# Layer norm inside a two-block network: squares about a provisional mean of four blocks, shifted by GpSimd while the last two blocks are made

## The chip, the cores and the metric

The kernel runs on one core of a Trainium2 chip. The metric is the time of one execution on the device, in microseconds (us). It is 1038.09 us, the median of 3 runs (1037.78 to 1038.72). The engines are named as the profile names them: PE is TensorE (PEld its weight loads), DVE is VectorE, ACT is ScalarE, POOL is GpSimd, SP is SyncE.

## The reference, cut to what matters

The program is a Conformer convolution block, a differential attention block with their SwiGLU and gate layers, and a second block of three branches, for 256 tokens of 1024 features in float32. The change lies in the convolution module of the first block, in its layer norm over the 1024 features:

```
def layer_norm(x, g, b):
    xf = x.astype(jnp.float32)
    mu = jnp.mean(xf, axis=-1, keepdims=True)
    xc = xf - mu
    var = jnp.mean(xc * xc, axis=-1, keepdims=True)
    y = xc * lax.rsqrt(var + EPS) * g.astype(jnp.float32) + b.astype(jnp.float32)
    return y.astype(x.dtype)

def conformer_conv(x, w_pw1, b_pw1, dw_w, dw_b, ln_g, ln_b, w_pw2, b_pw2):
    a = x @ w_pw1 + b_pw1
    u = a[..., :D_MODEL] * jax.nn.sigmoid(a[..., D_MODEL:])
    u = lax.conv_general_dilated(...)            # causal depthwise, 31 taps
    u = jax.nn.silu(layer_norm(u, ln_g, ln_b))
    return u @ w_pw2 + b_pw2
```

## The kernel before, in words

Every matrix product of float32 inputs is made of three products of rounded halves: `w_hi` and `w_lo` for a weight piece, `x_hi`, `x_lo` or `z_hi`, `z_lo` for the data (function `mm3`, lines L276 to L278). Weights come as 169 pieces of 1 MB, fetched by SP into `raw`, rounded by ACT into `w_hi` (L906) and subtracted by DVE into `w_lo` (L1388); for pieces 2 to 10 and two later ones POOL makes the low half (L795, `low`). The order of each engine is written out by hand, and engines wait for each other on counting semaphores.

In the convolution module the features lie on the 128 partitions, in 8 blocks of 128 features (f = 0 to 7), each block 256 tokens wide. Blocks 0 to 3 of the depthwise convolution are made by DVE, tap by tap (`taps_on_vector`, L1583 to L1594, the last add of a block is L1594). Blocks 4 to 7 are made by PE in four column strips of 32 (`conv_taps`, L476: 32 matmuls for a block, two recorded instructions each), and ACT copies them out with their bias (`conv_out`, L1057). All land in `y` (8 blocks).

The layer norm needs sums over the features, which lie on partitions, so PE makes them with a constant matrix `inv_d` (all 1/1024), which leaves the sum on all partitions. Before, this goes:

- POOL adds blocks 0, 1, 4 and 2 into `y_part`; PE multiplies `y_part` (L499) and blocks 5, 6, 3, 7 (`mean_of`, L486) into bank 0, which then holds the mean.
- DVE subtracts the mean from all of `y` in place, two blocks at a time (L1611).
- ACT squares `y` into `sq` (L1107); PE sums the squares in four column strips of bank 7 (L513); DVE copies them out to `y_sums` (L1615); two matmuls with one column turn the strips' sums into the variance of 128 tokens each (L521); DVE adds EPS (L1618); POOL raises to -0.5 (L835); DVE multiplies the identity by it (`y_diag`, L1621); PE spreads it over the partitions (`y_row`, L527).
- DVE multiplies `y` by that row (`scaled`, L1627), ACT applies gain, bias and SiLU (L1115) and rounds to `z_hi` (L1120), DVE makes `z_lo` (`v_split`, L1635). This runs over five groups of blocks, BLOCKS = (0), (1), (2,3), (4,5), (6,7).
- PE starts the second pointwise product (`by_feature`, piece 9) and waits ahead of each group for its `v_split`.

Between these steps PE does work that waits for nothing here: the four parts of the projection `proj0` (`projection_part`, two 128-row blocks of three matmuls each), and six transposes that nobody reads (`keep_warm`, L443). POOL, after `low(10)`, adds the bias row of the second product to `h` in four pieces of 128x512 (L827), starts the DMA of the attention bias (`toep`, L832), and then waits for the variance.

Of the kernel before, what the change touches and what calls it, by code (L numbers as in the profile page):

```python
# [77 lines left out]
def build(nc, ws, x_tok, p_feat, par, rows, lam_rows, rel, onehot, sgu_w, pool_m, toep, u_scr, out):  # L78
    ctx = ExitStack()
    with ctx:  # L80
# [46 lines left out]
        y_odd = view(9968, 2, SEQ)  # L127
        u_pad = view(2272, 7, PADDED)
# [120 lines left out]
        def _(pe):  # L249
# [30 lines left out]
            def tok(ap, k, t):  # L280
                return ap[:, k, t * P:(t + 1) * P]
# [61 lines left out]

            def projection_part(layer, g, b, t, n):

                begin(b)
                for k in range(2):
                    c = slice(k * D + n * 512, k * D + (n + 1) * 512)
                    ins = mm3(banks[b][:, :], tok(z_hi, KB - 2 + k, t), tok(z_lo, KB - 2 + k, t),
                              w_hi[:, g % SPLIT, c], w_lo[:, g % SPLIT, c], k == 0, k == 1)  # L350
                end(("proj", layer, t, n), b, ins, g if t == 1 and n == 1 else None)
# [128 lines left out]
            def mean_of(f, last=False):  # L480

                if f < CONV_PE:
                    pe.wait_ge(S("conv"), f + 1)
                else:
                    pe.wait_ge(S("conv_pe"), f - CONV_PE + 1)
# [10 lines left out]
            conv_taps(6)  # L496
# [3 lines left out]
            mean_of(5)  # L500
            conv_taps(7)
            mean_of(6)
            mean_of(3)
            mean_of(7, last=True)
            pe.wait_ge(S("p_split"), 1)
            lo_ready(pe, G["proj0"])
            for n in range(2):
                projection_part(0, G["proj0"], (1, 4)[n], 0, n)
            begin(7)
            for f in range(KB):  # L510
                pe.wait_ge(S("y_sq"), f // 2 + 1)
                j = f % QUADS
                ins = pe.matmul(banks[7][j * LANE:(j + 1) * LANE, 0:SEQ], inv_d[:, 0:LANE], sq[:, f, :],  # L513
                                start=f < QUADS, stop=f >= QUADS)
            end("squares", 7, ins, release=(S("y_sums"), 1))
            pe.wait_ge(S("y_sums"), 1)
            pe.wait_ge(S("one_32nd"), 1)
            begin(3)
            begin(2)
            for t, b in enumerate((3, 2)):  # L520
                end(("var", t), b, pe.matmul(banks[b][:, 0:1], y_sums[:, t * P:(t + 1) * P], one_32nd, start=True, stop=True),  # L521
                    release=(S("y_var"), t + 1))
            projection_part(0, G["proj0"], 5, 1, 0)
# [5 lines left out]
            projection_part(0, G["proj0"], 6, 1, 1)  # L529
            keep_warm(6, 7)  # L530
# [230 lines left out]
        def _(pool):  # L761
# [62 lines left out]
            for n_ in range(2):  # L824
                for t in range(TT):
                    c = slice(n_ * 512, (n_ + 1) * 512)
                    pool.tensor_tensor(h[:, t, c], h[:, t, c], row_b2[:, c], ALU.add).then_inc(S("h_biased"), 1)  # L827


            pool.wait_ge(S("bias_row"), 2)  # L830
            pool.wait_ge(S("ld_u0"), 128)
            pool.dma_start(toep, bias_row[:, :].unsqueeze(1).to_broadcast([HEADS, P, 384])).then_inc(S("toep_out"), 16)  # L832
            pool.memset(one_32nd, 1.0 / LANE).then_inc(S("one_32nd"), 1)
            pool.wait_ge(S("y_var"), 2)
            pool.tensor_tensor(st[:, 84:86], st[:, 82:84], st2[:, 56:58], ALU.pow).then_inc(S("y_r"), 1)  # L835
            pool.wait_ge(S("h_done"), 4)
# [59 lines left out]
        def _(act):  # L896
# [204 lines left out]
            spread(7)  # L1101
            conv_out(5)
            conv_out(6)
            conv_out(7)
            for f in range(4):
                act.wait_ge(S("centred"), f + 1)
                act.activation(sq[:, 2 * f:2 * f + 2, :], y[:, 2 * f:2 * f + 2, :], ACT.Square).then_inc(S("y_sq"), 1)  # L1107
# [263 lines left out]
        def _(dve):  # L1371
# [234 lines left out]
            bank, free = take(dve, "mean")  # L1606
            dve.wait_ge(S("conv_pe"), KB - CONV_PE)
            dve.wait_ge(S("conv"), CONV_PE)
            for i in range(4):
                k = slice(2 * i, 2 * i + 2)  # L1610
                dve.tensor_tensor(y[:, k, :], y[:, k, :], bank[:, 0:SEQ].unsqueeze(1).to_broadcast([P, 2, SEQ]),  # L1611
                                  ALU.subtract).then_inc(S("centred"), 1)
# [3 lines left out]
            for t in range(TT):  # L1616
                bank, free = take(dve, ("var", t))
                dve.tensor_scalar(st[:, 82 + t:83 + t], bank[:, 0:1], 1.0, EPS, ALU.mult, ALU.add).then_inc(S("y_var"), 1)  # L1618
# [4 lines left out]
            dve.wait_ge(S("centred"), 4)  # L1623

            def scaled(i):
                k = slice(*BLOCKS[i])
                dve.tensor_tensor(y[:, k, :], y[:, k, :],  # L1627
# [10 lines left out]
            for i in range(3):  # L1638
                scaled(i)
            v_split(0)  # L1640
# [451 lines left out]
```

## Time and profile before

| what | value |
|---|---|
| median of 3 runs | 1038.09 us (1037.78 to 1038.72) |
| the profiled execution | 1037.69 us, of which the span of instructions is 1035.9 us |
| PE busy | 1024.0 us, 99% |
| DVE busy | 640.8 us, 62% |
| ACT busy | 519.3 us, 50% |
| POOL busy | 107.8 us, 10% |
| granted clock of TensorE, mean | 0.999 |

The span counts from the first to the last instruction; the profiled execution has 1.8 us around it. Times in a timeline count from the start of the span. A row of the timeline may merge several instructions of one line (x3), and the durations of matmuls overlap, since they are pipelined: how far PE moves in a stretch is read from the start of one row to the start of the next. A number in square brackets is the idle time of the engine ahead of the row and what ended it.

### The profile page before, as it was taken

To read this page: it belongs to the slowest core of one execution; us is meant where nothing else is said; L and a number is where in the kernel's file an instruction comes from. 1 tells how busy PE (TensorE), PEld (TensorE's weight loads), DVE (VectorE), ACT (ScalarE), POOL (GpSimd) and SP (SyncE) were. 2 spreads that over 40 slices of the span, in tenths; PEclk is the share of its full clock that TensorE was granted. 3 is DMA by queue.
4 is the path that set the end of the run, shared out by engine and by line. 5 is a ranking of instruction groups with operands and counts; after the bars stand their busy time and mean duration, and the time that the engine had idled before them with its cause. 6 is when DMAs were issued, how large, how long until landed. Compare 5 with 4: busy or idle time off the path is not lost.

```text
span 1035.9 us, 13552 instructions
## 1 busy us (share of the span) xinstructions
PE 1024.0 (99%) x5530; PEld 865.2 (84%) x5530; DVE 640.8 (62%) x802; ACT 519.3 (50%) x635; POOL 107.8 (10%) x87
## 2 busy tenths in 40 slices
PE   8999999999999999999999999999999999999997
PEld 7977888888888888888888888788888888999886
DVE  5996745445457667765454456676454557777564
ACT  6337544434466668654434346754544454344433
POOL 4991100000020320010000002100000000000000
PEclk9999999999999999999999999999999999999999
DMA  8766865555453632565455554555545445454531
GB/s 311 254 186 129 259 224 191 192 179 197 174 192 122 230 137 82 204 225 202 175 191 196 177 196 163 210 202 214 198 179 190 159 163 203 172 195 164 205 120 41
DMA packets 30669, 191.67 MB, mean 185 GB/s; under 512 B 3720, under 2 KB 6280, under 8 KB 8720
## 3 DMA queue, kind: packets, MB, share of 16 engines
q1 hardware_dynamic: 25056, 179.06, 48.1%
q0 software_dynamic: 2096, 7.79, 3.3%
q10 hardware_dynamic: 3456, 3.97, 1.3%
q8 instruction: 44, 0.72, 0.3%
q14 instruction: 17, 0.14, 0.0%
HBM read 187.58 MB, written 3.21 MB: 184 GB/s over the span
## 4 chain that ended last, share of the span: by engine, by line
PE 98%; DVE 1%; ACT 0%; issue 0%; POOL 0%; POOLq 0%; ACTq 0%
PE bank L276 30%; PE bank L278 30%; PE bank L277 30%; PE bank L318 2%; PE bank L476 1%; PE bank L393 1%; PE bank L450 1%; PE bank L570 0%; PE bank L667 0%; PE bank L704 0%; DVE w_lo L1388 0%; PE bank L591 0%; PE bank L486 0%; DVE arena L1433 0%; DVE x_lo L1443 0%
## 5 line engine op out<-in xcount | busy, mean ns | idle before, releaser
L1388 DVE TENSOR_TENSOR w_lo<-raw,w_hi 128x2048 fp32r<-128x2048 f32 x158 | 361.7, 2292 | 210.9 <-ACT w_hi L906 210.6
L906 ACT ACTIVATE w_hi<-raw 128x2048 fp32r<-128x2048 f32 x169 | 322.7, 1910 | 162.3 <-PE bank L278 151.5
L276 PE MATMUL bank<-w_hi,x_hi 128*128 128x512 f32 x800 | 317.7, 397 | 0.2
L278 PE MATMUL bank<-w_hi,x_lo 128*128 128x512 f32 x800 | 312.5, 391 | 0.0
L277 PE MATMUL bank<-w_lo,x_hi 128*128 128x512 f32 x800 | 311.5, 389 | 0.0
L276 PEld LDWEIGHTS bank<-w_hi,x_hi 128*128 128x128 f32 x800 | 150.2, 188 | 34.4 <-issue 3.9
L278 PEld LDWEIGHTS bank<-w_hi,x_lo 128*128 128x128 f32 x800 | 150.1, 188 | 32.4
L277 PEld LDWEIGHTS bank<-w_lo,x_hi 128*128 128x128 f32 x800 | 150.4, 188 | 29.2
L276 PE MATMUL bank<-w_hi,z_hi 128*128 128x512 f32 (+1 forms) x368 | 143.4, 390 | 0.1
L278 PE MATMUL bank<-w_hi,z_lo 128*128 128x512 f32 (+1 forms) x368 | 141.7, 385 | 0.0
L277 PE MATMUL bank<-w_lo,z_hi 128*128 128x512 f32 (+1 forms) x368 | 141.5, 385 | 0.0
L276 PE MATMUL bank<-x_hi,w_hi 128*128 128x256 f32 x384 | 108.9, 284 | 1.5 <-DVE x_lo L1443 1.5
L277 PE MATMUL bank<-x_lo,w_hi 128*128 128x256 f32 x384 | 108.7, 283 | 0.0
L278 PE MATMUL bank<-x_hi,w_lo 128*128 128x256 f32 x384 | 108.7, 283 | 0.0
L795 POOL TENSOR_TENSOR w_lo<-raw,w_hi 128x2048 fp32r<-128x2048 f32 x11 | 51.1, 4650 | 370.1 <-ACT w_hi L906 370.1
L276 PEld LDWEIGHTS bank<-w_hi,z_hi 128*128 128x128 f32 x368 | 69.2, 188 | 14.1 <-issue 0.8
L278 PEld LDWEIGHTS bank<-w_hi,z_lo 128*128 128x128 f32 x368 | 69.1, 188 | 13.9
L277 PEld LDWEIGHTS bank<-w_lo,z_hi 128*128 128x128 f32 x368 | 69.2, 188 | 13.1
L276 PEld LDWEIGHTS bank<-x_hi,w_hi 128*128 128x128 f32 x384 | 73.7, 192 | 2.3 <-DVE x_lo L1443 1.1
L277 PEld LDWEIGHTS bank<-x_lo,w_hi 128*128 128x128 f32 x384 | 73.7, 192 | 0.0
L278 PEld LDWEIGHTS bank<-x_hi,w_lo 128*128 128x128 f32 x384 | 73.7, 192 | 0.0
L963 ACT ACTIVATE z_hi<-bank 128x512 fp32r<-128x512 f32 x22 | 13.1, 597 | 75.6 <-PE bank L393 75.6
(224 smaller groups left out, 757.6 us busy)
## 6 DMA issues: line engine op xcount, KB each, us to landing
raw<-in_ws SPq DMA_DIRECT2D x169, 1024.0 KB, 4.8
arena<-u_scr ACTq DMA_DIRECT2D x16, 142.0 KB, 4.6
arena<-in_rows POOLq DMA_DIRECT2D x2, 1024.0 KB, 5.1
toep<-bias_row POOLq DMA_DIRECT2D x1, 1536.0 KB, 34.4
h<-in_x_tok SPq DMA_DIRECT2D x2, 512.0 KB, 4.9
arena<-in_rows POOLq DMA_DIRECT2D x2, 512.0 KB, 5.9
arena<-toep POOLq DMA_DIRECT2D x1, 1024.0 KB, 11.0
arena<-in_pool_m POOLq DMA_DIRECT2D x1, 768.0 KB, 4.7
```

The lines of the kernel that those rows point to most:

```text
L276: pe.matmul(dst, s_hi, m_hi, start=first, stop=False)
L277: pe.matmul(dst, s_hi, m_lo, start=False, stop=False)
L278: return pe.matmul(dst, s_lo, m_hi, start=False, stop=last)
L318: ins = pe.transpose(banks[b][:, k * P:(k + 1) * P], src[:, k * P:(k + 1) * P], ident[:, :])
L393: ins = pe.transpose(banks[b][:, k * SEQ + t * P:k * SEQ + (t + 1) * P], hid[:, t, k * P:(k + 1) * P], ident[:, :])
L450: pe.matmul(banks[b][:, 0:P], ones[:, :], ident[:, :], start=True, stop=True)
L476: ins = pe.matmul(banks[b][j * LANE:(j + 1) * LANE, 0:SEQ], taps_of[:, i, q, j, :], u_rows[i % 3][:, j, 4 * q:4 * q + SEQ], start=q == 0, ...
L795: pool.tensor_tensor(w_lo[:, g % SPLIT, :], raw[:, g % RAW, :], w_hi[:, g % SPLIT, :].bitcast(F32), ALU.subtract).then_inc(S("lo_pool"), 1)
L906: act.activation(w_hi[:, g % SPLIT, :], raw[:, g % RAW, :], ACT.Copy).then_inc(hi_done, 1)
L963: act.activation(z_hi[:, k0:k0 + 2, :], bank[:, :].rearrange("p (k s) -> p k s", k=2), ACT.Copy).then_inc(S("t_hi"), 1)
L1388: dve.tensor_tensor(w_lo[:, g % SPLIT, :], raw[:, g % RAW, :], w_hi[:, g % SPLIT, :].bitcast(F32), ALU.subtract).then_inc(lo_done, 1)
```

## The change

The squares are no longer taken about the mean but about a pivot, and the difference is taken out afterwards. The pivot is the mean over four blocks: PE multiplies `y_part` twice (1/1024 each, over 512 features). ACT copies it to `pivot_row`. POOL subtracts it from blocks 0,1 then 2, then 4,5, then 6 (`shift`), DVE from 3 and 7. ACT squares each group as it is shifted. PE sums the shifted blocks (the mean of what is left, e, in bank 2) and the squares (bank 7), in an order that follows the shifts. The variance is the mean of squares less e squared: two more matmuls with one column (`e_cols`), a squaring on ACT and one DVE instruction that subtracts (`scalar_tensor_tensor`, two columns at once). DVE subtracts e from `y` (`centre`, four times) in between the later steps, instead of all ahead of the squares. POOL's four additions to `h` (`add_b2`) go from ahead of its power to behind it. `sq` lies at another place, `projection_part` is cut into steps of three matmuls, and `keep_warm` has 2 transposes for 6.

```
-        sq = view(6384, KB, SEQ)
+        sq = view(0, KB, SEQ)
...
-            def mean_of(f, last=False):
...
-                ins = pe.matmul(banks[0][:, 0:SEQ], inv_d, y[:, f, :], start=False, stop=last)
+            def mean_of(f, shifted, first=False, last=False):
+
+                pe.wait_ge(*shifted)
+                if first:
+                    begin(2)
+                ins = pe.matmul(banks[2][:, 0:SEQ], inv_d, y[:, f, :], start=first, stop=last)
                 if last:
-                    end("mean", 0, ins, release=(S("centred"), 4))
+                    end("mean", 2, ins, release=(S("centred"), 4))
+
+            def square_of(f, squared, last=False):
+
+                pe.wait_ge(S("y_sq"), squared)
+                j = f % QUADS
+                ins = pe.matmul(banks[7][j * LANE:(j + 1) * LANE, 0:SEQ], inv_d[:, 0:LANE], sq[:, f, :],
+                                start=f not in square_seen, stop=f in square_seen)
+                square_seen.update((f, (f + QUADS) % KB))
+                if last:
+                    end("squares", 7, ins, release=(S("y_sums"), 1))
...
             conv_taps(5)
-            conv_taps(6)
             begin(0)
             pe.wait_ge(S("y_part"), 1)
             pe.matmul(banks[0][:, 0:SEQ], inv_d, y_part, start=True, stop=False)
-            mean_of(5)
+            end("pivot", 0, pe.matmul(banks[0][:, 0:SEQ], inv_d, y_part, start=False, stop=True),
+                release=(S("shifted_v"), 2))
+            conv_taps(6)
             conv_taps(7)
-            mean_of(6)
-            mean_of(3)
-            mean_of(7, last=True)
             pe.wait_ge(S("p_split"), 1)
             lo_ready(pe, G["proj0"])
-            for n in range(2):
-                projection_part(0, G["proj0"], (1, 4)[n], 0, n)
+            projection_step(0, G["proj0"], 1, 0, 0, 0)
+            projection_step(0, G["proj0"], 1, 0, 0, 1)
+            mean_of(5, (S("shifted"), 3), first=True)
+            mean_of(6, (S("shifted"), 4))
             begin(7)
-            for f in range(KB):
...
+            square_of(0, 1)
+            square_of(1, 1)
+            square_of(2, 2)
+            square_of(4, 3)
+            square_of(5, 3)
+            square_of(6, 4)
+            mean_of(3, (S("shifted_v"), 1))
+            mean_of(7, (S("shifted_v"), 2), last=True)
+            square_of(3, 5)
+            square_of(7, 6, last=True)
+            projection_step(0, G["proj0"], 4, 0, 1, 0)
+            begin(0)
+            pe.wait_ge(S("e_row"), 1)
+            pe.wait_ge(S("one_32nd"), 1)
+            for t in range(TT):
+                ins = pe.matmul(banks[0][:, t:t + 1], e_row[:, t * P:(t + 1) * P], one_32nd, start=True, stop=True)
+            end("e_cols", 0, ins, release=(S("e_sq"), 1))
+            begin(3)
             pe.wait_ge(S("y_sums"), 1)
...
+            projection_step(0, G["proj0"], 4, 0, 1, 1)
+            projection_step(0, G["proj0"], 5, 1, 0, 0)
+            projection_step(0, G["proj0"], 5, 1, 0, 1)
             begin(3)
             pe.wait_ge(S("y_diag"), 2)
...
-            projection_part(0, G["proj0"], 6, 1, 1)
-            keep_warm(6, 7)
+            projection_step(0, G["proj0"], 6, 1, 1, 0)
+            projection_step(0, G["proj0"], 6, 1, 1, 1)
+            keep_warm(2, 7)
...
+            def shift(f0, f1):
+
+                pool.tensor_tensor(y[:, f0:f1, :], y[:, f0:f1, :], pivot_row.unsqueeze(1).to_broadcast([P, f1 - f0, SEQ]),
+                                   ALU.subtract).then_inc(S("shifted"), 1)
...
             low(10)
+            pool.wait_ge(S("pivot_row"), 1)
+            shift(0, 2)
+            shift(2, 3)
...
+            shift(4, 6)
...
+            shift(6, 7)
...
+            pool.wait_ge(S("y_var"), 1)
+            pool.tensor_tensor(st[:, 84:86], st[:, 82:84], st2[:, 56:58], ALU.pow).then_inc(S("y_r"), 1)
             pool.wait_ge(S("ld_b2"), 16)
             pool.wait_ge(S("x_scaled_1"), 1)
             pool.wait_ge(S("x_scaled"), 1)
...
+            add_b2(0)
+            add_b2(1)
...
+            square(0, 2, (S("shifted"), 1))
+            square(2, 3, (S("shifted"), 2))
             conv_out(7)
...
+            square(4, 6, (S("shifted"), 3))
+            square(6, 7, (S("shifted"), 4))
+            square(3, 4, (S("shifted_v"), 1))
+            square(7, 8, (S("shifted_v"), 2))
+            bank, _ = take(act, "mean")
+            act.activation(e_row, bank[:, 0:SEQ], ACT.Copy).then_inc(S("e_row"), 1)
+            bank, _ = take(act, "e_cols")
+            act.activation(st2[:, 50:52], bank[:, 0:TT], ACT.Square, scale=LANE / P).then_inc(S("e_sq"), 1)
             table(ACT.Silu)
```

On DVE the same part reads, in the changed kernel:

```
            dve.scalar_tensor_tensor(out=st[:, 82:84], in0=bank[:, 0:TT], scalar=EPS, in1=st2[:, 50:52], op0=ALU.add,
                                     op1=ALU.subtract).then_inc(S("y_var"), 1)
...
            centre(0)
            dve.wait_ge(S("y_r"), 1)
            for t in range(TT):
                dve.tensor_scalar(y_diag[:, t, :], ident[:, :], st[:, 84 + t:85 + t], None, ALU.mult).then_inc(S("y_diag"), 1)
            centre(1)
            row, free = take(dve, "y_row")
...
            for i in range(3):
                scaled(i)
            centre(2)
            v_split(0)
            scaled(3)
            centre(3)
            v_split(1)
            scaled(4)
```

How the instructions stand on the engines, row by row. PE before, from the sums of squares to the variance and the next projection matmuls (L513 squares, L521 variance):

```order
L513 MATMUL bank<-arena 32x256 x8
L521 MATMUL bank<-st,arena 128x1 x2
L276 MATMUL bank<-w_hi,z_hi 128x512
L277 MATMUL bank<-w_lo,z_hi 128x512
L278 MATMUL bank<-w_hi,z_lo 128x512
```

PE in the changed kernel, the same place (L492 sums of shifted blocks, L500 squares, L543 `e_cols`, L548 variance; lines are those of the changed kernel):

```order
L492 MATMUL bank<-arena 128x256 x2
L500 MATMUL bank<-arena 32x256 x6
L492 MATMUL bank<-arena 128x256 x2
L500 MATMUL bank<-arena 32x256 x2
L277 MATMUL bank<-w_hi,z_hi 128x512
L278 MATMUL bank<-w_lo,z_hi 128x512
L279 MATMUL bank<-w_hi,z_lo 128x512
L543 MATMUL bank<-st,arena 128x1 x2
L548 MATMUL bank<-st,arena 128x1 x2
```

The eight squares are cut into six and two with full-width sums between, and three projection matmuls and two one-column matmuls now stand ahead of the variance.

DVE before, from the last block of the convolution to the second `v_split`:

```order
L1594 TENSOR_TENSOR arena<-bank,arena 128x256
L1611 TENSOR_TENSOR arena<-arena,bank 128x512 x4
L1615 COPY arena<-bank 128x256
L1618 TENSOR_SCALAR st<-bank 128x1 x2
L1621 TENSOR_SCALAR arena<-ident,st 128x128 x2
L1627 TENSOR_TENSOR arena<-arena,bank 128x256 x2
L1627 TENSOR_TENSOR arena<-arena,bank 128x512
L1635 TENSOR_TENSOR z_lo<-arena,z_hi 128x256
L1627 TENSOR_TENSOR arena<-arena,bank 128x512
L1635 TENSOR_TENSOR z_lo<-arena,z_hi 128x256
```

DVE in the changed kernel (L1670, L1672 subtract the pivot, L1681 is `centre`, L1694 `y_diag`, L1701 `scaled`, L1709 `v_split`):

```order
L1670 TENSOR_TENSOR arena<-arena,bank 128x256
L1672 TENSOR_TENSOR arena<-arena,bank 128x256
L1675 COPY arena<-bank 128x256
L1686 SCALAR_TENSOR_TENSOR st<-bank,st 128x2
L1681 TENSOR_TENSOR arena<-arena,bank 128x512
L1694 TENSOR_SCALAR arena<-ident,st 128x128 x2
L1681 TENSOR_TENSOR arena<-arena,bank 128x512
L1701 TENSOR_TENSOR arena<-arena,bank 128x256 x2
L1701 TENSOR_TENSOR arena<-arena,bank 128x512
L1681 TENSOR_TENSOR arena<-arena,bank 128x512
L1709 TENSOR_TENSOR z_lo<-arena,z_hi 128x256
L1701 TENSOR_TENSOR arena<-arena,bank 128x512
```

The third subtraction of a mean now stands ahead of the first `v_split`, the fourth (not shown) ahead of the second.

POOL before, behind the third addition to `y_part` (L795 is `low(10)`, L827 the additions to `h`, L835 the power):

```order
L795 TENSOR_TENSOR w_lo<-raw,w_hi 128x2048
L827 TENSOR_TENSOR h<-h,arena 128x512 x4
L832 DMA toep<-bias_row 1024x1x384
L833 MEMSET st 128x1
L835 TENSOR_TENSOR st<-st 128x2
```

POOL in the changed kernel (L825 is `low(10)`, L859 `shift`, L876 the power, L855 `add_b2`):

```order
L825 TENSOR_TENSOR w_lo<-raw,w_hi 128x2048
L859 TENSOR_TENSOR arena<-arena 128x512
L859 TENSOR_TENSOR arena<-arena 128x256
L859 TENSOR_TENSOR arena<-arena 128x512
L859 TENSOR_TENSOR arena<-arena 128x256
L873 DMA toep<-bias_row 1024x1x384
L876 TENSOR_TENSOR st<-st 128x2
L855 TENSOR_TENSOR h<-h,arena 128x512 x4
```

The four shifts take the place of the four additions, and the additions now start where the power ends.

## Rows read from the trace of the kernel before

**Rows 1.** The page, the chain that ended last, shares of the span

```profile
PE 98%; DVE 1%; ACT 0%; issue 0%; POOL 0%; POOLq 0%; ACTq 0%
```

**Rows 2.** Stretches: us, busy (instructions) of PE, PEld, DVE, ACT, POOL, then PEclk, DMA

```profile
0.00:40.00 40.00, 35.99 (x280) 34.50 (x281) 27.85 (x53) 21.48 (x22) 24.29 (x22) 1.00 0.82 288
...
82.00:90.00 8.00, 7.30 (x48) 5.16 (x47) 4.20 (x11) 5.77 (x11) 0.83 (x2) 1.00 0.49 52
```

**Rows 3.** Timeline of PE around the layer norm: start, us, what

```profile
79.43 1.68 PE L486 MATMUL bank<-arena 128*128 128x256 f32 x6
80.76 0.58 PE L276 MATMUL bank<-w_hi,z_hi 128*128 128x512 f32 x1
...
83.77 1.21 PE L513 MATMUL bank<-arena 128*32 128x256 f32 x16
85.50 0.61 PE L521 MATMUL bank<-st,arena 128*128 128x1 f32 x4 [0.53 <-DVE arena L1615]
85.97 0.47 PE L276 MATMUL bank<-w_hi,z_hi 128*128 128x512 f32 x1
...
87.78 0.68 PE L527 MATMUL bank<-arena,ones 128*128 128x128 f32 x4 [0.18 <-DVE arena L1621]
88.22 0.48 PE L276 MATMUL bank<-w_hi,z_hi 128*128 128x512 f32 x1
...
89.68 0.82 PE L443 MATMUL bank<-ident 128*128 128x128 f32 x6
90.64 0.47 PE L276 MATMUL bank<-w_hi,z_hi 128*128 128x512 f32 x1
```

**Rows 4.** Timeline of DVE around the layer norm

```profile
79.50 0.42 DVE L1594 TENSOR_TENSOR arena<-bank,arena 128x256 f32<-128x256 f32 x1
81.15 2.48 DVE L1611 TENSOR_TENSOR arena<-arena,bank 128x512 f32<-128x512 f32 x4 [1.22 <-PE bank L486]
...
87.15 0.48 DVE L1621 TENSOR_SCALAR arena<-ident,st 128x128 f32<-128x128 f32 x2 [0.85 <-POOL st L835]
88.50 1.35 DVE L1627 TENSOR_TENSOR arena<-arena,bank 128x256 f32<-128x256 f32 x3 [0.86 <-PE bank L527]
90.11 0.43 DVE L1635 TENSOR_TENSOR z_lo<-arena,z_hi 128x256 fp32r<-128x256 f32 x1 [0.26 <-ACT z_hi L1120]
...
91.05 0.43 DVE L1635 TENSOR_TENSOR z_lo<-arena,z_hi 128x256 fp32r<-128x256 f32 x1
```

**Rows 5.** Timeline of POOL around the layer norm and after it

```profile
75.89 5.00 POOL L827 TENSOR_TENSOR h<-h,arena 128x512 f32<-128x512 f32 x4
...
86.39 0.73 POOL L835 TENSOR_TENSOR st<-st 128x2 f32<-128x2 f32 x1 [4.29 <-DVE st L1618]
...
118.20 0.72 POOL L849 TENSOR_TENSOR st<-st 128x2 f32<-128x2 f32 x1
```

**Rows 6.** Timeline of ACT behind the first block scaled

```profile
88.95 0.60 ACT L1115 ACTIVATE arena<-arena,prm 128x256 f32<-128x256 f32 x1 [2.17 <-DVE arena L1627]
```

**Rows 7.** Timeline of DVE at 8, 118 and 341 us

```profile
8.99 2.30 DVE L1548 TENSOR_SCALAR arena<-h,st 128x1024 f32<-128x1024 f32 x1 [7.11 <-POOL st L783]
...
118.27 1.29 DVE L1443 TENSOR_TENSOR x_lo<-arena,x_hi 128x512 fp32r<-128x512 f32 x2
...
340.84 2.29 DVE L1388 TENSOR_TENSOR w_lo<-raw,w_hi 128x2048 fp32r<-128x2048 f32 x1
```

**Rows 8.** Timeline of POOL at 8 us

```profile
8.11 0.73 POOL L783 TENSOR_TENSOR st<-st 128x2 f32<-128x2 f32 x1
8.83 4.23 POOL L787 TENSOR_TENSOR arena<-arena,prm 128x1024 f32<-128x1024 f32 x2
```

**Rows 9.** One line each: duration in ns, min/median/max, first and last start

```profile
L787 POOL TENSOR_TENSOR arena<-arena,prm x4: 1904/1929/2356, 8.8 to 55.7; 128x1024 f32<-128x1024 f32 x4
L858 POOL TENSOR_SCALAR arena<-st x4: 204/208/2207, 341.0 to 384.9; 128x16 f32<-128x16 f32 x4
L1960 DVE TENSOR_SCALAR arena<-arena,st x1: 486/486/486, 1032.2 to 1032.2; 128x512 f32<-128x512 f32 x1
```

More of the change, by code:

```diff
@@ L509, in _ @@
+            projection_step(0, G["proj0"], 1, 0, 0, 1)
+            mean_of(5, (S("shifted"), 3), first=True)
+            mean_of(6, (S("shifted"), 4))
             begin(7)
-            for f in range(KB):
[L511 to L515, printed above, removed]
@@ L516, in _ @@
-            pe.wait_ge(S("y_sums"), 1)
[L517 to L523, printed above, removed]
+            square_of(0, 1)
+            square_of(1, 1)
+            square_of(2, 2)
+            square_of(4, 3)
@@ L524, in _ @@
+            end("e_cols", 0, ins, release=(S("e_sq"), 1))
+            begin(3)
+            pe.wait_ge(S("y_sums"), 1)
+            for t in range(TT):
+                ins = pe.matmul(banks[3][:, t:t + 1], y_sums[:, t * P:(t + 1) * P], one_32nd, start=True, stop=True)
+            end("var", 3, ins, release=(S("y_var"), 1))
+            projection_step(0, G["proj0"], 4, 0, 1, 1)
+            projection_step(0, G["proj0"], 5, 1, 0, 0)
+            projection_step(0, G["proj0"], 5, 1, 0, 1)
             begin(3)
@@ L823, in _ @@
             pool.wait_ge(S("x_scaled"), 1)
[L824 to L835, printed above, removed]
+            add_b2(0)
+            add_b2(1)
             pool.wait_ge(S("h_done"), 4)
@@ L1101, in _, with square @@
             spread(7)
+            bank, _ = take(act, "pivot")
+            act.activation(pivot_row, bank[:, 0:SEQ], ACT.Copy).then_inc(S("pivot_row"), 1)
             conv_out(5)
             conv_out(6)
-            conv_out(7)
-            for f in range(4):
-                act.wait_ge(S("centred"), f + 1)
-                act.activation(sq[:, 2 * f:2 * f + 2, :], y[:, 2 * f:2 * f + 2, :], ACT.Square).then_inc(S("y_sq"), 1)
+            def square(f0, f1, shifted):
+                act.wait_ge(*shifted)
+                act.activation(sq[:, f0:f1, :], y[:, f0:f1, :], ACT.Square).then_inc(S("y_sq"), 1)
+            square(0, 2, (S("shifted"), 1))
+            square(2, 3, (S("shifted"), 2))
+            conv_out(7)
+            square(4, 6, (S("shifted"), 3))
[6 more added lines that the diff above has]
+            act.activation(st2[:, 50:52], bank[:, 0:TT], ACT.Square, scale=LANE / P).then_inc(S("e_sq"), 1)
             table(ACT.Silu)
@@ L1605, in _ @@
             taps_on_vector(3, {4: lambda: gated(7)})
-            bank, free = take(dve, "mean")
+            bank, free = take(dve, "pivot")
+            dve.wait_ge(S("pivot_row"), 1)
+            dve.wait_ge(S("conv"), CONV_PE)
+            dve.tensor_tensor(y[:, 3, :], y[:, 3, :], bank[:, 0:SEQ], ALU.subtract).then_inc(S("shifted_v"), 1)
             dve.wait_ge(S("conv_pe"), KB - CONV_PE)
[L1608 to L1612, printed above, removed]
+            dve.tensor_tensor(y[:, 7, :], y[:, 7, :], bank[:, 0:SEQ], ALU.subtract).then_inc(S("shifted_v"), 1)
             feed(9)
@@ L1615, in _, with centre @@
             dve.tensor_copy(y_sums, bank[:, 0:SEQ]).then_inc(S("y_sums"), 1)
-            for t in range(TT):
-                bank, free = take(dve, ("var", t))
-                dve.tensor_scalar(st[:, 82 + t:83 + t], bank[:, 0:1], 1.0, EPS, ALU.mult, ALU.add).then_inc(S("y_var"), 1)
+            e_bank, _ = take(dve, "mean")
+            def centre(i):
+                k = slice(2 * i, 2 * i + 2)
+                dve.tensor_tensor(y[:, k, :], y[:, k, :], e_bank[:, 0:SEQ].unsqueeze(1).to_broadcast([P, 2, SEQ]),
+                                  ALU.subtract).then_inc(S("centred"), 1)
+            bank, free = take(dve, "var")
+            dve.wait_ge(S("e_sq"), 1)
+            dve.scalar_tensor_tensor(out=st[:, 82:84], in0=bank[:, 0:TT], scalar=EPS, in1=st2[:, 50:52], op0=ALU.add,
+                                     op1=ALU.subtract).then_inc(S("y_var"), 1)
+            dve.wait_ge(S("e_row"), 1)
+            dve.wait_ge(S("shifted"), 4)
+            dve.wait_ge(S("shifted_v"), 2)
+            centre(0)
             dve.wait_ge(S("y_r"), 1)
```

32 lines of the change are left out of this document (22 added, 10 removed).

## The prediction

> **What bounds the kernel now.** I read the page first, its chain of work that ended last: 98% of the span is PE [rows 1]. So the time changes only where PE's own work changes or where PE waits, and the change lies in one stage, from 79.43 us (PE has finished the convolution) to 90.64 us (PE starts the second pointwise product) [rows 3]. The reader is to see how little PE loses there: it is busy 7.30 of the 8.00 us between 82 and 90 [rows 2]. It waits 0.53 us for the copy of the sums of squares, 0.18 us at `y_row`, and from 89.68 to 90.64 us, 0.96 us, it runs the filler transposes and then waits for the first `v_split`, which ends at 90.11 + 0.43 = 90.54 us [rows 3, 4]. With all of PE's idle time in 82 to 90 (0.70 us) the stage has at most 0.70 + 0.96 = 1.7 us to give. That is under 0.2% of 1038 us (2.1 us), which is about what a measurement of this kernel can tell from no change. So the question is mostly what the change adds. Last I read POOL and DVE side by side, since POOL's work is moved.
>
> **The pivot and the shifts.** Two matmuls for the pivot stand where `y_part` and block 5 stood, so block 7 of the convolution still ends near 79.43 us. Behind `low(10)` POOL makes four shifts. The additions took 5.00 / 4 = 1.25 us for 128x512, from 75.89 us [rows 5]; I take 1.25 for a shift of two blocks and 0.75 for one, so the last ends at 75.9 + 4.0 = 79.9 us. DVE ends block 3 at 79.92 us [rows 4] and shifts blocks 3 and 7, 0.42 each, by 80.8. ACT's squares (0.6 for two blocks) follow by 81.8. PE wants the last of these only after 83 us (below). All this is hidden, with over 1 us of cover. POOL's DMA `toep` starts 0.9 us earlier, with a reader far away: hidden.
>
> **PE from 79.43 us to `y_row`.** Sums of blocks: three took 80.76 - 79.43 = 1.33 us, so four take 1.77. Projection: still 18 matmuls ahead of `y_row`, twelve at 83.77 - 80.76 = 3.01 us and six at 89.68 - 88.22 = 1.46: 4.47. Squares: a full-width sum is two recorded halves of 1.33 / 6 = 0.22 us. Eight in four strips took 1.21 us with their tail, their sixteen halves started over 0.83 us, so a strip takes 0.22 a half and four strips run side by side. Now six run in three strips (four halves deep, 0.89 us) and two, blocks 3 and 7, in one and the same strip (four halves one behind the other, 0.89 us): 1.78. `e_cols` and the variance: 85.97 - 85.50 = 0.47 each, 0.94. Four more changes between strips and full width: twelve projection matmuls between two other kinds took 0.09 us more than twice six, so 0.36. The sum is 9.32 us, `y_row` at 88.75 us against 87.78 [rows 3]: 0.97 later. If the one strip costs nothing extra and the changes are free, it is 1.25 less. The waits of PE are gone, but they were 0.7 us, and the added work is more.
>
> **The variance chain, without POOL's other work.** `y_row` less nine projection matmuls (2.19) less 0.47 puts the variance at 86.09 us. Before, POOL's power started 86.39 - 85.50 = 0.89 us behind it and took 0.73, DVE started 0.03 later and took 0.48 for both `y_diag` [rows 3 to 5]. So: power 86.98 to 87.71 us, `y_diag` until 88.22, PE could start at 88.37, and its own queue (88.75) ends later. `centre(0)` lies under the power. ACT has 2.17 us of idle ahead of the first SiLU [rows 6]; its table load and copies move 2 us later and just fit.
>
> **What POOL now does beside `y_diag`.** This is the step I rest the forecast on. The four additions to `h` now start right behind the power, the moment in which `y_diag` starts on DVE. The same meeting stands in the trace at 8.8 us: a power ends (L783), POOL goes straight on to L787, and DVE starts L1548, released by that same power [rows 7, 8]. L1548 takes 2.30 us for 128x1024. The same operation takes 0.486 us for 128x512, late in the program with POOL idle, and POOL's first L787 ends at about 8.83 + 1.9 = 10.7 us; DVE's instruction ends at 11.29 [rows 7 to 9]. So it stood still until POOL's had ended and then ran 0.55 us. The second L787 took 2.36 us where the median is 1.93, so POOL in turn waited for DVE [rows 9]. It happens the other way too: L858 takes 0.2 us, and 2.21 where it started inside DVE's L1388, which has two inputs in SBUF and ends at 343.13 us, as L858 does within 0.1 [rows 7, 9]. Against it stands one row: DVE's L1443 at 118.27 us, two SBUF inputs, started inside POOL's power L849 and was not delayed (1.29 for two) [rows 5, 7]; but a power of 2 columns reads almost nothing.
>
> The Trainium skill, page "SBUF — State Buffer", section "SBUF: two separate sides", states that VectorE and GpSimd share a port pair as an exclusive lock for a whole instruction, for a VectorE operation in a 2-port mode or with two SBUF inputs. The trace agrees at 8.8 and 341 us, and not at 118 us. By the page the sum is the one that follows; by the row at 118 us alone it would be the first rival's.
>
> With it: POOL's first addition starts at 87.7 us and ends at 88.97. The first `y_diag` ends 0.15 us later, about 89.1. POOL's second addition is already queued and takes its turn, until 90.37; the second `y_diag` ends at 90.5, PE's `y_row` starts at 90.67. From `y_row` to the second product it was 90.64 - 87.78 = 2.86 us. `centre(2)` (2.48 / 4 = 0.62) now stands ahead of the first `v_split`, of which 0.35 lay idle from one start to the next: 0.27 more. PE starts the product at 93.80, 3.16 us later. The second `v_split` came 91.05 - 90.11 = 0.94 us behind the first, now 1.56 with `centre(3)`, against 1.4 of PE's work: about 0.1 more [rows 3, 4]. Later ones have slack. Sum 3.2 us. If both `y_diag` slip in behind the first addition, `y_row` is at 89.45, the first `v_split` is wanted at 92.04 and meets the fourth addition (until 93.05): product at 93.45, 2.8 us. I take 3.0. Behind the stage PE is never short of work for 300 us, so nothing is given back.
>
> Made against the profiled execution, 1037.69 us (1035.9 of span and 1.8 around it), this gives 1040.7; that execution lies 0.4 under the median of 1038.09, so I forecast **1041.1 us**.
>
> **The rivals.**
> *No meeting of POOL and DVE* (this is the other side, no slower that can be told). Then `y_row` is at 88.75, the product at 88.75 + 2.86 + 0.27 = 91.88, 1.24 later, and 1.35 with the second `v_split`: 1039.4. For it: the row at 118 us, and that POOL's loop may start its reads after DVE's short instruction (128 columns) is through. It decides whenever both `y_diag` and the `v_split`s end unstretched.
> *Only the `v_split`s meet it.* Both `y_diag` win, at 88.2; the additions then end at 89.5, 90.7, 92.0 and 93.2, the first `v_split` (wanted at 91.34) ends at 92.3, the second behind the fourth: 1.9 us, 1040.0.
> *PE's added work is smaller than counted.* The strip of blocks 3 and 7 packs as before and the changes are free: the product at about 90.7, 1038.1. Against it: strips run side by side only with each other.
> *Slower still*: PE idles about 1.9 us at `y_row` and 1 us ahead of the product, with 2 transposes for 6, and the granted clock falls. Against it: over the first 40 us PE is idle 4.0 us and the granted clock is 1.00 [rows 2]. A microsecond of PE's work at the lower level costs one more; I allow 1043 and up.
>
> **How the numbers follow.** Forecast 0.55, `v_split`s only 0.12, no meeting 0.18, less work 0.09, slower still 0.06. The forecast's own range is 1040.3 to 1041.9 (2.8 to 3.2 and 0.5 either way between runs). The 8-in-10 range reaches down past the no-meeting case and leaves out the less-work and slower-still cases: 1038.8 to 1042.2. Slower by over 0.2% (over 1040.2): nearly all of the forecast, half of the `v_split` case, the last: 0.62. Faster by over 0.2% cannot come from 1.7 us: 0.02. Within: 0.36.
>
> **What would show it.** In the changed kernel's profile: block 7 of the convolution ends within 0.1 of 79.4; the two squares of one strip start over 0.66 us; the power starts near 87.0; the first `y_diag` does not take 0.28 us but about 1.3, and the pair ends near 90.5; PE has an idle time ahead of `y_row` (1.9 us, released by DVE) and one ahead of the product; additions of POOL over 1.3 us. I am wrong if the two `y_diag` take 0.48 us together, or if PE is not released by DVE at the product.

## The result, and the profile after

The changed kernel takes 1040.67 us, the median of 13 runs (1040.45 to 1042.64), against 1037.92 us for the kernel before (13 runs, 1037.68 to 1038.72). The ratio is 1.0026, with a 95% interval of 1.0019 to 1.0033: slower by about 2.7 us. Forecast were 1041.1 us and a chance of 0.62 for slower.

The profiled execution took 1040.83 us, its span 1039.0 us. PE's timeline around the layer norm (L492 sums of shifted blocks, L500 squares, L543 `e_cols`, L548 variance, L556 `y_row`, L450 filler; compare [rows 3]):

```profile
79.86 0.50 PE L277 MATMUL bank<-w_hi,z_hi 128*128 128x512 f32 x1
...
81.35 1.03 PE L492 MATMUL bank<-arena 128*128 128x256 f32 x4
82.30 1.06 PE L500 MATMUL bank<-arena 128*32 128x256 f32 x12
83.30 1.13 PE L492 MATMUL bank<-arena 128*128 128x256 f32 x4
...
84.36 1.05 PE L500 MATMUL bank<-arena 128*32 128x256 f32 x4
85.34 0.50 PE L277 MATMUL bank<-w_hi,z_hi 128*128 128x512 f32 x1
...
86.51 0.58 PE L548 MATMUL bank<-st,arena 128*128 128x1 f32 x4
...
88.87 0.39 PE L279 MATMUL bank<-w_hi,z_lo 128*128 128x512 f32 x1
90.89 0.68 PE L556 MATMUL bank<-arena,ones 128*128 128x128 f32 x4 [1.64 <-DVE arena L1694]
...
94.00 0.47 PE L277 MATMUL bank<-w_hi,z_hi 128*128 128x512 f32 x1 [0.81 <-issue]
```

The convolution ends at 79.86 us in this execution and at 79.43 in that of before, though the code up to there does the same work. The 0.43 us between them arose earlier: PE starts the first of the four blocks of its column strips (`conv_taps`) at 52.43 us before and at 52.86 now, and from there to the convolution's end both take 27.00 us. So all places below are counted from the end of the convolution, and I call the start of the second product there "the product". It stood 11.21 us behind the convolution before and stands 94.00 - 79.86 = 14.14 us behind it now: 2.93 us more. The reader is to see two waits: 1.64 us ahead of `y_row`, which DVE's L1694 ends, and 0.81 us ahead of the product. The profile names no releaser for the second (`issue`), but it is the wait for the first `v_split`: that ends at 93.48 + 0.42 = 93.90 us and PE starts 0.10 us later, as before (90.54 and 90.64), and PE follows the `v_split` wherever the experiments move it (93.10 and 93.20 us in the first, 91.85 and 91.94 in the second). The first wait is the `y_diag` pair. DVE and POOL in the same stretch (compare [rows 4, 5]; L1694 is `y_diag`, L1681 `centre`, L1701 `scaled`, L1709 `v_split`, L876 the power, L855 the additions):

```profile
87.20 0.16 DVE L1686 SCALAR_TENSOR_TENSOR st<-bank,st 128x2 f32<-128x2 f32 x1 [1.32 <-PE bank L548]
...
88.21 2.54 DVE L1694 TENSOR_SCALAR arena<-ident,st 128x128 f32<-128x128 f32 x2 [0.19 <-POOL st L876]
90.67 0.67 DVE L1681 TENSOR_TENSOR arena<-arena,bank 128x512 f32<-128x512 f32 x1
91.61 1.35 DVE L1701 TENSOR_TENSOR arena<-arena,bank 128x256 f32<-128x256 f32 x3 [0.27 <-PE bank L556]
92.88 0.68 DVE L1681 TENSOR_TENSOR arena<-arena,bank 128x512 f32<-128x512 f32 x1
93.48 0.42 DVE L1709 TENSOR_TENSOR z_lo<-arena,z_hi 128x256 fp32r<-128x256 f32 x1
```

```profile
87.45 0.73 POOL L876 TENSOR_TENSOR st<-st 128x2 f32<-128x2 f32 x1 [6.12 <-DVE st L1686]
88.15 4.99 POOL L855 TENSOR_TENSOR h<-h,arena 128x512 f32<-128x512 f32 x4
```

The two `y_diag` take 2.54 us where they took 0.48 [rows 4]. POOL's first addition starts 0.06 us ahead of them. The `scaled` and `centre` instructions, which read one operand from PSUM, run beside the additions at their old durations. The additions take what they took (4.99 against 5.00), and end at 93.14 us, before the first `v_split`.

### The profile page after: what moved, and what is told of

Same layout as the page of the kernel before. It is cut to its first block, busy times and chain, and to the rows that moved or that the text cites. A ratio compares the mean times of both kernels' runs of the same rounds, so it can differ in the third digit from the quotient of the medians.

```text
span 1039.0 us, 13569 instructions
## 1 busy us (share of the span) xinstructions
PE 1025.5 (99%) x5532; PEld 866.5 (83%) x5532; DVE 643.0 (62%) x803; ACT 520.1 (50%) x640; POOL 111.6 (11%) x91
## 4 chain that ended last, share of the span: by engine, by line
PE 96%; issue 1%; DVE 1%; POOL 1%; ACT 1%; POOLq 0%; ACTq 0%
PE bank L277 30%; PE bank L279 30%; PE bank L278 30%; PE bank L319 2%; PE bank L400 1%; PE bank L457 1%; PE bank L600 0%; POOL w_lo L825 0%; PE bank L483 0%; PE bank L697 0%; PE bank L734 0%; POOL arena L859 0%; DVE w_lo L1449 0%; PE bank L621 0%; DVE arena L1494 0%
## 5 line engine op out<-in xcount | busy, mean ns | idle before, releaser
L825 POOL TENSOR_TENSOR w_lo<-raw,w_hi 128x2048 fp32r<-128x2048 f32 x11 | 51.0, 4644 | 371.6 <-ACT w_hi L952 371.5
```

Source lines behind the costliest of these rows:

```text
L825: pool.tensor_tensor(w_lo[:, g % SPLIT, :], raw[:, g % RAW, :], w_hi[:, g % SPLIT, :].bitcast(F32), ALU.subtract).then_inc(S("lo_pool"), 1)
```

## The experiments

The theory (the **port theory**): a DVE instruction that needs the SBUF port it shares with POOL (one whose tensor operands all lie in SBUF, as in `y_diag` and `v_split`) stands still until POOL's running instruction ends; that, and not the pivot scheme, makes most of the loss. Its main rival: PE's added work makes it. A second: the stall is a fixed delay, or holds whatever follows POOL's power. All edits are to the changed kernel unless it is said otherwise, and all kernels compute the whole reference.

| kernel | product behind the convolution, us | median, us | ratio to before (95%) |
|---|---|---|---|
| before | 11.21 | 1037.92 | |
| changed | 14.14 | 1040.67 | 1.0026 (1.0019 to 1.0033) |
| 1 additions behind `y_diag` | 13.16 | 1039.77 | 1.0012 (1.0003 to 1.0021) |
| 2 additions behind `v_split`s | 12.28 | 1038.94 | 1.0003 (0.9995 to 1.0012) |
| 3 additions of 256 | 13.58 | 1040.08 | 1.0009 (1.0000 to 1.0018) |
| 4 additions of 1024 | 16.80 | 1044.11 | 1.0051 (1.0034 to 1.0068) |
| 5 `y_diag` on ACT | 12.48 | 1039.75 | 1.0015 (1.0005 to 1.0024) |
| 6 as 2, two strips | 11.85 | 1038.41 | 1.0001 (0.9992 to 1.0010) |
| 7 before, additions moved | 13.25 | 1040.78 | 1.0027 (1.0016 to 1.0038) |
| 8 built to win | 11.12 | 1038.48 | 1.0007 (0.9998 to 1.0016) |
| 9 identity from PSUM | 12.52 | 1039.49 | 1.0012 (1.0003 to 1.0021) |
| 10 as 4, PE kept warm | 16.34 | 1043.44 | 1.0046 (1.0034 to 1.0059) |

The first column is from one profile each, the others from repeated runs. Each ratio is to runs of the kernel before made beside that kernel (medians 1038.44 us for kernels 1 to 4, 1038.16 for 5 to 8, 1038.41 for 9 and 10), and is not the ratio of the medians shown. Those runs of before scattered from 1037.6 to 1041.6, so for steps of a few tenths the first column tells more. The medians of kernels 4, 5, 7 and 8 lie 1.3, 0.75, 0.8 and 0.7 us above their forecasts, though except in the fourth the product stands within 0.1 us of where it was forecast. In the profiles of the fourth and the eighth the convolution ends 0.5 and 0.6 us later than in the changed kernel (80.37 and 80.47 against 79.86), which lies ahead of the stage; why it does, and what adds to the fifth and the seventh, is open.

**1. The additions wait for `y_diag`.**

```
+            pool.wait_ge(S("y_diag"), 2)
             add_b2(0)
             add_b2(1)
```

> The changed kernel, but POOL's four additions to h wait until both y_diag are made. Port theory (a DVE operation in a 2-port mode or with two SBUF inputs stands still while POOL works through an addition): the two y_diag take 0.48 us together instead of 2.54, PE starts y_row from its own queue, 9.25 us behind the end of the convolution instead of 11.04, and the additions now meet the first v_split, which ends up to 0.8 us late. Second product 13.0 us behind the convolution (changed kernel 14.15, before 11.21): about 1.15 us less than the changed kernel, 1039.5. If v_splits are not held: 12.35 us and 1038.9. Rival (PE's added work is what costs): as the changed kernel, 1040.7.

DVE and POOL (L1695 `y_diag`, L1710 `v_split`):

```profile
88.41 0.48 DVE L1695 TENSOR_SCALAR arena<-ident,st 128x128 f32<-128x128 f32 x2 [0.19 <-POOL st L876]
...
91.21 0.68 DVE L1682 TENSOR_TENSOR arena<-arena,bank 128x512 f32<-128x512 f32 x1
91.81 1.29 DVE L1710 TENSOR_TENSOR z_lo<-arena,z_hi 128x256 fp32r<-128x256 f32 x1
93.03 0.67 DVE L1702 TENSOR_TENSOR arena<-arena,bank 128x512 f32<-128x512 f32 x1
```

```profile
89.06 5.20 POOL L855 TENSOR_TENSOR h<-h,arena 128x512 f32<-128x512 f32 x4 [0.69 <-DVE arena L1695]
```

The product comes at 13.16 us, forecast 13.0. `y_diag` is back at 0.48 us, and now it is the first `v_split` that is held: 1.29 us for 0.42. It has two inputs in SBUF; `centre` and `scaled` before and behind it, with one input in PSUM, are not held (0.68, 0.67). The Trainium skill, page "SBUF — State Buffer", section "SBUF: two separate sides", names both kinds, an operation in a 2-port mode and one with two SBUF inputs; the trace agrees, with 2.54 us for the `y_diag` pair of the changed kernel and 1.29 us for this `v_split`.

**2. The additions wait for all `v_split`s.**

```
+            pool.wait_ge(S("v_split"), len(BLOCKS))
             add_b2(0)
             add_b2(1)
```

> The changed kernel, but the four additions wait until all five v_splits are made, so that they meet nothing on the way to the second product. Port theory: y_diag 0.48 us for both, v_split 0.42, second product 12.35 us behind the convolution, 1.8 us less than the changed kernel: 1038.9; what is left over the kernel before (about 1 us) is PE's added work and the two centres ahead of v_splits. Rival (PE's added work is the whole cost): 1040.7.

12.28 us and 1038.94: as the theory said, and not to be told from the kernel before. So the meeting is 14.14 - 12.28 = 1.86 of the 2.93 us. POOL's additions now meet DVE's L1450, the `w_lo` subtraction with two SBUF inputs, and both stretch:

```profile
97.99 11.30 POOL L855 TENSOR_TENSOR h<-h,arena 128x512 f32<-128x512 f32 x4 [10.00 <-DVE z_lo L1710]
```

```profile
98.86 2.58 DVE L1450 TENSOR_TENSOR w_lo<-raw,w_hi 128x2048 fp32r<-128x2048 f32 x1 [1.04 <-ACT w_hi L953]
101.64 3.10 DVE L1450 TENSOR_TENSOR w_lo<-raw,w_hi 128x2048 fp32r<-128x2048 f32 x1 [0.20 <-ACT w_hi L953]
```

The additions take 11.30 us for 5, the subtractions 2.58 and 3.10 for 2.29 [rows 7], and PE waits for none of it: the same stall costs nothing where there is cover.

**3 and 4. The size of the additions.**

```
-                    c = slice(n_ * 512, (n_ + 1) * 512)
-                    pool.tensor_tensor(h[:, t, c], h[:, t, c], row_b2[:, c], ALU.add).then_inc(S("h_biased"), 1)
+                    for q in range(2):
+                        c = slice(n_ * 512 + q * 256, n_ * 512 + (q + 1) * 256)
+                        pool.tensor_tensor(h[:, t, c], h[:, t, c], row_b2[:, c], ALU.add).then_inc(S("h_biased"), 1)
```

> The changed kernel with the additions cut into eight of 128x256 (about 0.73 us each by the additions to y_part) at the same place. Port theory: each y_diag ends about 0.09 us behind one addition, so the pair takes about 1.5 us instead of 2.54 and the second product comes 0.9 us earlier: 1039.8. Rival (a fixed delay, whatever the length of POOL's instruction): 2.54 us again and 1040.7.

The fourth kernel has `pool.tensor_tensor(h[:, n_, :], h[:, n_, :], row_b2, ALU.add)` for each half, two in all.

> The changed kernel with the additions as two of 128x1024 (2.3 us each by the 4.6 us of 128x2048) at the same place. Port theory: the second y_diag ends behind the second addition, the pair takes about 4.7 us, y_row and the product come 2.1 us later than in the changed kernel: 1042.8. Rival (a fixed delay): 1040.7.

`y_diag` and the additions of the third kernel, then `y_diag` of the fourth:

```profile
87.89 1.46 DVE L1695 TENSOR_SCALAR arena<-ident,st 128x128 f32<-128x128 f32 x2 [0.19 <-POOL st L877]
...
92.08 0.93 DVE L1710 TENSOR_TENSOR z_lo<-arena,z_hi 128x256 fp32r<-128x256 f32 x1
```

```profile
87.83 5.77 POOL L856 TENSOR_TENSOR h<-h,arena 128x256 f32<-128x256 f32 x8
```

```profile
88.73 4.69 DVE L1692 TENSOR_SCALAR arena<-ident,st 128x128 f32<-128x128 f32 x2 [0.20 <-POOL st L874]
```

The pair takes 1.46, 2.54 and 4.69 us with additions of 0.72, 1.25 and 2.33 us: two additions each time, and no fixed delay. The totals missed. In the third the first `v_split` was wanted inside an addition and took 0.93 us, which I had not counted: 13.58 for some 13.25 us. In the fourth the product came 0.5 us later than the pair explains, which is the tenth experiment's question; most of the rest of the 1.3 us that its median missed by lies ahead of the stage, as said above.

**5. `y_diag` on ACT**, the additions where they were.

```
+            act.wait_ge(S("y_r"), 1)
+            for t in range(TT):
+                act.activation(y_diag[:, t, :], ident[:, :], ACT.Copy, scale=st[:, 84 + t:85 + t]).then_inc(S("y_diag"), 1)
```

> The changed kernel with POOL's additions left where they are, right behind the power, but the two y_diag made by ACT (Copy with a scale) instead of DVE. Port theory (the stall is between DVE and POOL alone): ACT's two take about 0.6 us, y_row starts from PE's queue near 9.25 us behind the convolution, the second product at about 12.4 us (the first v_split may still meet the third addition for 0.2 us), 1039.0. Rival (POOL's additions hold whoever touches these tiles, or delay the power's release): ACT's y_diag take 2.5 us too, 1040.7.

```profile
87.95 0.68 ACT L1172 ACTIVATE arena<-ident,st 128x128 f32<-128x128 f32 x2
```

ACT reads the same tiles inside the same addition and is not held: 0.68 us for both, product at 12.48. So neither the power's release nor the tiles are what waits. The median is 0.75 us above the forecast; in the profile 0.4 of it lies behind the product (945.6 us to the end of the span, 945.2 in most others), and I have no cause for that.

**6. The squares of blocks 3 and 7 in two strips**, on the second kernel.

```
-                j = f % QUADS
+                j = {0: 0, 1: 1, 2: 2, 4: 3, 5: 0, 6: 1, 3: 2, 7: 3}[f]
```

> The kernel of the second experiment (additions behind the v_splits) with the squares of blocks 3 and 7 in two different strips instead of one. If PE's queue is what sets y_row once the meeting is gone, the last two squares start over 0.24 us instead of 0.67 and everything behind is 0.43 us earlier: product 11.85 us behind the convolution against 12.28, 1038.5. If PE's queue does not set it, 12.28 and 1038.9.

```profile
84.01 0.63 PE L500 MATMUL bank<-arena 128*32 128x256 f32 x4
84.56 0.50 PE L277 MATMUL bank<-w_hi,z_hi 128*128 128x512 f32 x1
```

From the squares to the next projection matmul it is 0.55 us, against 85.34 - 84.36 = 0.98 in the changed kernel; the product moves by the same 0.43. With the meeting gone, PE's queue sets `y_row`.

**7. The move alone, in the kernel before**: its four additions behind the power, nothing else changed.

```
             pool.tensor_tensor(st[:, 84:86], st[:, 82:84], st2[:, 56:58], ALU.pow).then_inc(S("y_r"), 1)
+            for n_ in range(2):
+                for t in range(TT):
+                    c = slice(n_ * 512, (n_ + 1) * 512)
+                    pool.tensor_tensor(h[:, t, c], h[:, t, c], row_b2[:, c], ALU.add).then_inc(S("h_biased"), 1)
```

> The kernel before with one part of the change alone: the four additions to h stand behind the power instead of behind low(10). Port theory: both y_diag take 2.5 us instead of 0.48, y_row and the second product come 2.05 us later (product 13.25 us behind the convolution against 11.21): 1040.0. Rival (the cost is in the pivot scheme, PE's added work and the centres): as before, 1037.9.

```profile
87.67 2.52 DVE L1619 TENSOR_SCALAR arena<-ident,st 128x128 f32<-128x128 f32 x2 [0.85 <-POOL st L826]
```

```profile
90.34 0.68 PE L527 MATMUL bank<-arena,ones 128*128 128x128 f32 x4 [2.21 <-DVE arena L1619]
```

With this one move the old kernel's product comes at 13.25 us, 2.04 later than before, as forecast, and no pivot is in it. The median, 1040.78 us, is 0.8 above the forecast of 1040.0 and as high as that of the whole change. The seven runs scatter from 1040.31 to 1043.67 and the interval, 1.0016 to 1.0038, holds both 2.04 us and more, so the share of the move is taken from the profile.

**8. A version built to win**: the sixth kernel, with this order on PE, and on DVE `centre` 0 to 2 in idle time and 3 behind the second `v_split`.

```
             square_of(7, 6, last=True)
-            projection_step(0, G["proj0"], 4, 0, 1, 0)
...
+            projection_step(0, G["proj0"], 4, 0, 1, 0)
             projection_step(0, G["proj0"], 4, 0, 1, 1)
             projection_step(0, G["proj0"], 5, 1, 0, 0)
-            projection_step(0, G["proj0"], 5, 1, 0, 1)
...
+            projection_step(0, G["proj0"], 5, 1, 0, 1)
             projection_step(0, G["proj0"], 6, 1, 1, 0)
             projection_step(0, G["proj0"], 6, 1, 1, 1)
-            keep_warm(2, 7)
```

> A version built to win: additions behind the v_splits, two strips for blocks 3 and 7, e_cols and the variance directly behind the squares, one projection step moved behind y_row, centres 0 to 2 in DVE's idle time ahead of the power and y_row, centre 3 behind the second v_split, no filler transposes. Counted: y_row 8.2 us behind the convolution, first v_split done at 11.0, second product at 11.1 us against 11.21 before: 1037.8, not to be told from the kernel before. If a step was missed, up to 12.0 us and 1038.7.

The product stands 11.12 us behind the convolution, 0.09 ahead of before, as counted. The median of 1038.48 us missed its forecast of 1037.8, and the ratio, 1.0007 (0.9998 to 1.0016), can't be told from 1. No version here beats the kernel before.

**9. The identity read from PSUM**, the additions where they were.

```
+            ins = pe.transpose(banks[0][:, P:2 * P], ident[:, :], ident[:, :])
...
-                dve.tensor_scalar(y_diag[:, t, :], ident[:, :], st[:, 84 + t:85 + t], None, ALU.mult).then_inc(S("y_diag"), 1)
+                dve.tensor_scalar(y_diag[:, t, :], i_bank[:, P:2 * P], st[:, 84 + t:85 + t], None, ALU.mult).then_inc(S("y_diag"), 1)
```

> The changed kernel, POOL's additions right behind the power as there, and y_diag still on DVE, but its input, the identity, is read from PSUM (one more transpose on PE puts it there, 0.11 us). Port theory: DVE no longer needs what POOL holds, the two take about 0.55 us instead of 2.54, y_row starts near 9.4 us behind the convolution, the first v_split (two inputs in SBUF) may be held 0.1 us, product at 12.5 us, 1039.2. Rival (any DVE instruction that starts just behind POOL's addition is held, whatever it reads): 2.5 us and 1040.7.

```profile
88.53 0.61 DVE L1696 TENSOR_SCALAR arena<-bank,st 128x128 f32<-128x128 f32 x2 [0.26 <-POOL st L877]
...
91.87 0.59 DVE L1711 TENSOR_TENSOR z_lo<-arena,z_hi 128x256 fp32r<-128x256 f32 x1
```

```profile
88.41 5.21 POOL L856 TENSOR_TENSOR h<-h,arena 128x512 f32<-128x512 f32 x4
```

The same DVE instruction, started 0.12 us behind the same addition, takes 0.61 us for two instead of 2.54, with its input in PSUM and its output still in SBUF. So it is the place of the input that decides whether `y_diag` is held, and not the moment at which it starts. Whether the read itself needs what POOL holds, or a faster way of working that DVE uses only from SBUF to SBUF, isn't shown: the pair takes 0.48 us from SBUF with POOL idle and 0.61 here, so the two need not run in the same way. The product came at 12.52 us.

**10. The fourth kernel with PE kept busy** while it waits (`keep_warm(26, 7)` ahead of the wait for `y_diag`).

> The kernel of the fourth experiment (two additions of 128x1024) with 26 filler transposes on PE ahead of its wait for y_diag, 2.9 us at 0.11 each, so that PE idles about 1 us instead of 3.8. If the extra 0.5 us of that kernel between y_row and the second product (3.61 against 3.11 in the changed kernel) is the lower granted clock behind the idle time, the clock stays at 1.00, y_row is where it was (13.2 us behind the convolution), the product comes 3.1 us behind it, 0.5 us earlier, 1043.6. If the clock has no part in it, 3.6 us and 1044.1.

`y_row` and the first `scaled` of the fourth kernel, then stretches of the fourth and of the tenth (the third number from the right is the granted clock):

```profile
93.56 1.19 PE L556 MATMUL bank<-arena,ones 128*128 128x128 f32 x4 [3.79 <-DVE arena L1692]
```

```profile
94.79 1.35 DVE L1699 TENSOR_TENSOR arena<-arena,bank 128x256 f32<-128x256 f32 x3 [0.78 <-PE bank L556]
```

```profile
92.00:94.00 2.00, 0.43 (x2) 0.47 (x3) 2.00 (x2) 0.00 (x0) 1.33 (x1) 0.79 0.47 48
94.00:96.00 2.00, 2.00 (x8) 1.71 (x8) 1.22 (x4) 0.72 (x2) 0.00 (x0) 0.50 0.49 51
96.00:98.00 2.00, 2.00 (x10) 1.50 (x9) 2.00 (x5) 1.97 (x5) 0.00 (x0) 0.86 0.51 53
```

```profile
92.00:94.00 2.00, 1.29 (x8) 1.19 (x9) 1.73 (x4) 0.11 (x1) 0.48 (x1) 1.00 0.47 48
94.00:96.00 2.00, 1.17 (x7) 0.80 (x6) 2.00 (x5) 1.94 (x5) 0.00 (x0) 1.00 0.45 46
```

The product comes 3.11 us behind `y_row` instead of 3.61, and the clock stays at 1.00. The half microsecond was the clock, and it was lost in the `y_row` matmuls: `scaled` starts 94.79 - 93.56 = 1.23 us behind their start, in the changed kernel 91.61 - 90.89 = 0.72. The projection matmuls behind them were slow too, but that fell into PE's wait for the `v_split`.

## Why the prediction was right

**The bound, and what the stage could give.** Right. From the product to the end of the span it is 945.3 us before, 945.0 after, and 945.1 to 945.6 in the ten experiments: what the stage loses is lost, to within 0.3 us. Of the 1.7 us that the stage was said to have at most, the best version gained 0.09.

**The pivot and the shifts.** Right, hidden. ACT ends the last square at 81.90 us and PE takes up the last two blocks at 84.36; PE runs from 79.86 to 89.1 us without a wait.

**PE's work to `y_row`.** The variance was forecast 6.66 us behind the convolution and stands at 86.51 - 79.86 = 6.65. PE's queue would have reached `y_row` at about 9.25 us (the last projection matmul starts at 88.87), forecast 9.32. The single strip was as counted: its four halves are alone on PE (84.36 to 85.34 us), and the sixth experiment takes 0.43 us of it away.

**The meeting of `y_diag` with POOL's additions.** The step that decided, and right: two additions, one ahead of each `y_diag`. `y_row` was forecast at 11.24 us and came at 11.03. The term was too large by 0.2, because I had DVE's turn push POOL's next addition by 0.15 each time; the additions in fact ran on unstretched (4.99 us), and each `y_diag` ended about 0.09 behind one. The mark that I named, additions over 1.3 us, was wrong with it (the longest took 1.28): it holds for a `v_split`, with 256 columns and two inputs where a `y_diag` has 128 and one (5.20 for the four in the first experiment). Runs show when DVE is held and when not; that the cause is a port is the theory that fits them.

**From `y_row` to the product.** 3.13 forecast, 3.11 measured. The 0.1 for the second `v_split` is there for a moment (PE's next group starts at 95.48 us and its second matmul at 95.82, 0.34 us where 0.23 is usual) and is not left in the time behind the product. The sum of the order of events that happened was 3.2; I took 3.0, the middle between it and an order that did not happen. The profile has 2.93 and the medians 2.75, so that the number lies this close is in part luck. The forecast of 1041.1 lies 0.43 above 1040.67: 0.25 by this step and 0.17 because the kernel before came out at 1037.92 for 1038.09.

**The other marks.** The power started at 87.45 - 79.86 = 7.59 us behind the convolution, forecast 7.6, and the first `y_diag` took 1.31 us, forecast about 1.3. The convolution did not end within 0.1 of 79.4 us but at 79.86, for a reason that lies ahead of 52.86 us. PE is released by DVE at the product, though the profile's row says `issue` there.

**The rivals.** No meeting, 1039.4: what the second experiment shows when the meeting is taken away, 12.28 us and 1038.94; forecast for that case was a product at 91.88 - 79.43 = 12.45. `v_split`s only, 1040.0: that is the first experiment, 13.16 us and 1039.77. Less work on PE: fell, the work is as counted. The row at 118 us that spoke against the meeting was a power on two columns. The trace of before has a stronger one, with a power on 16 columns (L859) that takes 2.90 us:

```profile
351.29 2.90 POOL L859 TENSOR_TENSOR st<-arena,st 128x16 f32<-128x16 f32 x1
```

```profile
351.55 2.29 DVE L1388 TENSOR_TENSOR w_lo<-raw,w_hi 128x2048 fp32r<-128x2048 f32 x1 [0.65 <-ACT w_hi L906]
```

DVE's subtraction has two inputs in SBUF, starts and ends inside the power, and takes its usual 2.29 us. So not every instruction of POOL holds DVE for as long as it runs. That a power holds the port only while it reads its few columns is my reading and wasn't tried by itself. Falling clock: not at 1.64 us of idle time; it came only in the fourth experiment. The row set against it, 4.0 us of idle time in the first 40, was weak, since it is 2.1 us ahead of PE's first instruction and 1.9 us in three later waits of at most 0.9 us each, and not one wait.

**The shares.** Of 2.93 us the meeting is 1.86 (second experiment) and the scheme itself 1.07, of which 0.43 is the shared strip (sixth). In the kernel before the same move costs 2.04 us (seventh), since there `y_diag` sets `y_row` and has no cover behind PE's queue.

## What to carry to other kernels

When work is moved to another place on GpSimd, look at what VectorE does in that moment. A subtraction of two SBUF tensors, or a scaling from SBUF to SBUF, waited here until GpSimd's running addition ended, however short it was itself, and each one of a pair waited for an addition of its own. GpSimd's power on a few columns held nothing. Three ways out cost little here: put the GpSimd work behind a later semaphore, give the short instruction to ScalarE, or let it read PSUM; cutting GpSimd's instruction only bounds the wait. And before filling waits with reordered work, count what the reordering adds: here 0.7 us of PE's waits ahead of `y_row` were removed with 1.6 us more of PE's work (8.35 us with the waits before, 9.25 without any in the first experiment), and even the best order gained 0.09 us.

## What was not expected of the hardware

- The granted clock fell to its lower level, 0.50 or 1.2 GHz, in the fourth experiment, where PE had idled 3.79 us. It stayed at 1.00 where PE had idled 1.64 us (changed kernel) and 2.21 us (seventh). The `y_row` matmuls behind the long wait took 1.19 us instead of 0.68, the first projection matmuls 0.77 and 0.63 instead of 0.48 and 0.39.
- An addition of POOL is not stretched by a `y_diag` of 128 columns that waits behind it, but a `v_split` of 256 columns with two inputs costs POOL about 0.2 us (5.20 to 5.23 for four in three kernels).
- The convolution ended between 79.43 and 80.47 us in the twelve profiles, with the same work ahead of it. All of the difference had arisen when PE began the first of its four blocks of the convolution, at 52.43 to 53.47 us; from there to the end it is 27.00 us in each of them. A stage must be measured from its own start before its tenths mean anything.
